# Differential attention scores as three fp32r passes instead of fp32 matmuls

## The reference

```
s = jnp.einsum('bqhcd,bkhcd->bhcqk', qblk, kk, preferred_element_type=jnp.float32) * scale
p = jax.nn.softmax(s, axis=-1)
a = p[:, :, 0] - lam_full * p[:, :, 1]
return jnp.einsum('bhqk,bkhe->bqhe', a.astype(v.dtype), v)
```

## Time and profile before

| | |
|---|---|
| median of three runs | 3787.01 us |
| the profiled execution | 3786.81 us |
| its span | 3785.0 us |
| TensorE matmuls busy | 3628.1 us, 96% |
| VectorE busy | 1748.2 us, 46% |
| ScalarE busy | 1507.0 us, 40% |
| GpSimd busy | 1277.0 us, 34% |
| first score block of the first paired layer | starts at 1882.92 us |
| first score block of the second paired layer | starts at 2849.29 us |

### The profile page before, as it was taken

One profiled execution on the slowest core, in us unless ns is written; L12 is line 12 of the kernel. 1 busy time (PEld: TensorE's weight loads), 2 busy tenths in 40 slices (PEclk: granted clock), 3 DMA queues, 4 the chain that ended last, 5 costly groups with the idle time before them and its releaser, 6 DMA issues.

```text
span 3785.0 us, 53305 instructions
## 1 busy us (share of the span) xinstructions
PE 3628.1 (96%) x19978; PEld 2921.6 (77%) x19978; DVE 1748.2 (46%) x2548; ACT 1507.0 (40%) x2525; POOL 1277.0 (34%) x540
## 2 busy tenths in 40 slices
PE   7999999999988889999999999899989999999998
PEld 5875788888866767888777778688867777877886
DVE  4766643333356655443555552511156555252114
ACT  4343432222355654332555552422235555333222
POOL 2530333222331112444423334344433333434443
PEclk9999999999999999999999999999999999999999
DMA  5358211111210001322211122222222122222222
GB/s 205 117 218 303 80 67 61 62 66 61 78 56 23 23 23 67 106 94 96 99 62 67 63 72 95 73 101 98 96 78 73 68 68 68 87 86 85 98 95 89
DMA packets 84708, 333.82 MB, mean 88 GB/s; under 512 B 9520, under 2 KB 9648, under 8 KB 78000
## 3 DMA queue, kind: packets, MB, share of 16 engines
q1 hardware_dynamic: 83808, 329.22, 24.9%
q10 hardware_dynamic: 720, 2.10, 0.2%
HBM read 329.18 MB, written 2.10 MB: 88 GB/s over the span
## 4 chain that ended last, share of the span: by engine, by line
PE 78%; issue 11%; DVE 6%; POOL 3%; ACT 2%; POOLq 0%; DVEq 0%; ACTq 0%
PE pB L276 16%; PE pB L277 16%; PE pB L278 16%; PE pB L2327 13%; POOL w_lo L2892 3%; PE pO L276 1%; PE pO L278 1%; PE pO L277 1%; PE pT L278 1%; PE pT L277 1%; PE pT L276 1%; PE pT L2385 1%; DVE arena L903 1%; DVE small L1975 1%; PE pO L2412 1%
## 5 line engine op out<-in xcount | busy, mean ns | idle before, releaser
L2892 POOL TENSOR_TENSOR w_lo<-w_raw,w_hi 128x1024 fp32r<-128x1024 f32 x520 | 1260.7, 2426 | 2356.7 <-ACT w_hi L322 2356.3
L276 PE MATMUL pB<-h_hi,w_hi 128*128 128x512 f32 x2084 | 822.7, 395 | 43.0 <-DVE h_lo L2820 15.3
L277 PE MATMUL pB<-h_lo,w_hi 128*128 128x512 f32 x2084 | 817.2, 392 | 0.0
L278 PE MATMUL pB<-h_hi,w_lo 128*128 128x512 f32 x2084 | 816.2, 392 | 0.0
L322 ACT ACTIVATE w_hi<-w_raw 128x1024 fp32r<-128x1024 f32 x520 | 547.8, 1054 | 479.9 <-PE pB L278 315.0
L276 PEld LDWEIGHTS pB<-h_hi,w_hi 128*128 128x128 f32 x2084 | 395.2, 190 | 137.0 <-issue 39.1
L278 PEld LDWEIGHTS pB<-h_hi,w_lo 128*128 128x128 f32 x2084 | 395.1, 190 | 83.5
L277 PEld LDWEIGHTS pB<-h_lo,w_hi 128*128 128x128 f32 x2084 | 395.4, 190 | 79.9 <-issue 0.7
L276 PE MATMUL pB<-b_hi,w_hi 128*128 128x512 f32 (+1 forms) x1088 | 403.3, 371 | 6.4 <-POOL w_lo L2892 6.4
L277 PE MATMUL pB<-b_lo,w_hi 128*128 128x512 f32 (+1 forms) x1088 | 398.3, 366 | 0.0
L278 PE MATMUL pB<-b_hi,w_lo 128*128 128x512 f32 (+1 forms) x1088 | 397.9, 366 | 0.0
(11 more groups left out here) (546 smaller groups left out, 5223.7 us busy)
## 6 DMA issues: line engine op xcount, KB each, us to landing
w_raw<-stream SPq DMA_DIRECT2D x520, 512.0 KB, 3.2
under<-ada SPq DMA_DIRECT2D x42, 1024.0 KB, 4.8
arena<-ada SPq DMA_DIRECT2D x6, 1024.0 KB, 17.6
x<-xT SPq DMA_DIRECT2D x1, 2048.0 KB, 8.5
out<-x SPq DMA_DIRECT2D x8, 256.0 KB, 2.1
xc<-cT SPq DMA_DIRECT2D x1, 1024.0 KB, 26.5
arena<-bmask ACTq DMA_DIRECT2D x1, 1024.0 KB, 4.8
arena<-brope ACTq DMA_DIRECT2D x2, 256.0 KB, 5.1
```

Source lines behind the costliest of these rows:

```text
L276: pe.matmul(dst, lh, rh, start=(begin and k == 0), stop=False)
L277: pe.matmul(dst, lh, rl, start=False, stop=False)
L278: last = pe.matmul(dst, ll, rh, start=False, stop=(end and k == len(pairs) - 1))
L2892: pool.tensor_tensor(w_lo[:, s, :], w_raw[:, s, :], w_hi[:, s, :].bitcast(F32), ALU.subtract).then_inc(lo_ready, 1)
```

## The change

- **Scores.** For a differential turn `pe_scores` makes, for both 64-row halves, three fp32r passes instead of one fp32 matmul: high q x high k, remainder q x high k, high q x remainder k. In block 0 it waits for `score_hi` before the first pass and for `score_lo` before the second and once more before the third, so that the key's remainder is needed last.
- **High parts.** `act_score_high`, a ScalarE copy that rounds 512 columns to fp32r. For queries it stands at the head of `act_chunk` of the key chunk, ahead of the swap (`split_behind`). For keys it stands behind chunk 1 (turn 0) or behind `act_turned` of block 3 of the turn before (turns 2, 4, 6), and waits for the rotation.
- **Remainders.** `dve_score_low`, a VectorE subtraction with both inputs in SBUF, in place over `qr` and `kr`. For queries it stands at the head of `dve_rope` of the key chunk, ahead of the rotation; for keys at its end.
- `score_parts` is a view of the arena with fp32r type; no memory is added. There are 16 of each new ScalarE and VectorE operation (2 layers, 4 turns, q and k). No DMA changes.

```diff
--- before.py
+++ after.py
@@ -164,6 +164,8 @@
         with nc.sbuf_tensor("arena", [P, ARENA], F32) as arena:
             pass
         with nc.sbuf_tensor("mla_under", [P, 5376], F32), nc.sbuf_tensor("mla_q", [P, 4, T], F32R) as mla_q, nc.sbuf_tensor("mla_k", [P, 4, TC], F32R) as mla_k:
+            pass
+        with nc.sbuf_tensor("score_under", [P, 3072], F32), nc.sbuf_tensor("score_parts", [P, 12, T], F32R) as score_parts:
             pass
         xh_hi, xh_lo = sb("xh_hi", [P, KD * C], F32R), sb("xh_lo", [P, KD * C], F32R)
         xb_hi, xb_lo = sb("xb_hi", [P, KD * C], F32R), sb("xb_lo", [P, KD * C], F32R)
@@ -2270,6 +2272,27 @@
         V_NO = [sum(kind(c)[0] == "v" for c in range(k)) for k in range(PAIR_CHUNKS)]
         N_ROPES, N_VS = 32, 16
+        def splits(k):
+            return k < PAIR_CHUNKS and kind(k)[0] != "v" and kind(k)[1] == 0 and diff(TURN_OF[k])
+        SPLIT_NO = [sum(splits(c) for c in range(k)) for k in range(PAIR_CHUNKS)]
+        N_SPLITS = sum(splits(k) for k in range(PAIR_CHUNKS))
+        def score_halves(u):
+            at = 1 if diff(u) else 2
+            return [(score_parts[:, w * 6 + at, :], score_parts[:, w * 6 + u % 2 * 3, :]) for w in range(2)]
+        def split_behind(k):
+            return [j for j in range(max(k - 2, 0), k) if splits(j) and TURN_OF[j] == TURN_OF[k]
+                    and not split_alone(j) and next(c for c in range(j + 1, PAIR_CHUNKS) if kind(c)[0] != "v") == k]
+        def split_alone(k):
+            return diff(TURN_OF[k]) and kind(k)[0] == "k"
         def turn_start(u):
             at = turn_chunks(u)[0] + turn_chunks(u)[1] if u < TURNS else PAIR_CHUNKS + EARLY - 1
@@ -2312,6 +2335,7 @@
         pair_s, pair_m, pair_e, pair_c, pair_t = sem("pair_s"), sem("pair_m"), sem("pair_e"), sem("pair_c"), sem("pair_t")
         pair_ca, pair_cd, pair_v, pair_o = sem("pair_ca"), sem("pair_cd"), sem("pair_v"), sem("pair_o")
+        score_hi, score_lo = sem("score_hi"), sem("score_lo")
         swapped, rope_step, vfm_ready, gates_ready = sem("swapped"), sem("rope_step"), sem("vfm_ready"), sem("gates_ready")
@@ -2347,14 +2371,22 @@
             first, cnt = turn_chunks(u)
             if t == 0:
                 pe.wait_ge(rope_done, l * N_ROPES + ROPE_NO[first + 2 * cnt // 3 - 1] + 1)
+                parts_ready = l * N_SPLITS + sum(splits(k) for k in range(first + cnt))
+                if diff(u):
+                    pe.wait_ge(score_hi, parts_ready)
             if n and diff((n - 1) // TB % TURNS):
                 pe.wait_ge(pair_e, n)
             elif n:
                 pe.wait_ge(pair_m, n)
             q, k = qr[par], kr[par]
+            (qh, ql), (kh, kl) = score_halves(u)
+            passes = ((qh, kh, True, False), (ql, kh, False, False), (qh, kl, False, True))
             if diff(u):
-                for c in range(2):
-                    last = pe.matmul(pS[:, each(c)], q[halves(c), 0, t * P:(t + 1) * P], k[halves(c), 0, :], start=True, stop=True)
+                for i, (q_, k_, begin, end) in enumerate(passes):
+                    if t == 0 and i:
+                        pe.wait_ge(score_lo, parts_ready - 2 + i)
+                    for c in range(2):
+                        last = pe.matmul(pS[:, each(c)], q_[halves(c), t * P:(t + 1) * P], k_[halves(c), :], start=begin, stop=end)
             else:
                 near = ((0, t * P, (t + 2) * P),) if t + 1 < TB else ((0, t * P, T), (P, 0, P))
                 for o, a, b in near:
@@ -2462,6 +2494,8 @@
             if k >= PAIR_CHUNKS:
                 act.activation(sg[k - PAIR_CHUNKS], bank[s][:, :], ACT.Copy).then_inc(evac[s], 1)
             elif kind(k)[0] != "v":
+                for j in split_behind(k):
+                    act_score_high(act, l, j)
                 r = l * N_ROPES + ROPE_NO[k]
                 if r >= 2:
                     act.wait_ge(rope_done, r - 1)
@@ -2482,6 +2516,13 @@
                 act.activation(win[:, 0, 0], by_half[:, 1, TB - 1], ACT.Copy).then_inc(vfm_ready, 1)
             act_hi_part(act, g + SLOTS)
+        def act_score_high(act, l, k):
+            u = TURN_OF[k]
+            w = "qk".index(kind(k)[0])
+            act.wait_ge(rope_done, l * N_ROPES + ROPE_NO[k] + 1)
+            act.activation(score_halves(u)[w][0], (qr, kr)[w][u % 2][:, 0, :], ACT.Copy).then_inc(score_hi, 1)
         def act_values(act, l, k):
             s = (G_DIFF[l] + k) % SLOTS
             act.wait_ge(v_turned, l * N_VS + V_NO[k] + 1)
@@ -2534,6 +2575,8 @@
         def act_pairs(act, l):
             for k in range(FIRST):
                 act_chunk(act, l, k)
+                if splits(k) and split_alone(k):
+                    act_score_high(act, l, k)
             act_exps(act, l, 0, 0)
             for u in range(TURNS):
                 for t in range(TB):
@@ -2552,6 +2595,9 @@
                     if u and t == finish_at(u - 1):
                         act_finish(act, l, u - 1)
                     act_turned(act, l, u, t)
+                    if t + 1 == TB and put_off(u):
+                        for k in ropes_in(in_part(u, t - 1, 1)):
+                            act_score_high(act, l, k)
                     if t + 1 < TB:
                         act_exps(act, l, u, t + 1)
                     elif u + 1 < TURNS and not late(u + 1):
@@ -2575,6 +2621,8 @@
             dst = (qr if what == "q" else kr)[u % 2][:, gi, :]
             windowed = what == "k" and gi == 0 and not diff(u)
             to = knat if windowed else dst
+            for j in split_behind(k):
+                dve_score_low(dve, l, j)
             dve.wait_ge(swapped, r + 1)
             dve.tensor_tensor(to, bank[s][:, :], cos2, ALU.mult).then_inc(evac[s], 1)
             dve.tensor_tensor(qsw[r % 2], qsw[r % 2], sin2, ALU.mult).then_inc(rope_step, 1)
@@ -2588,6 +2636,16 @@
                 dve.tensor_tensor(win[:, 0, 0], a[:, 1, TB - 1], b[:, 1, TB - 1], ALU.add).then_inc(rope_done, 1)
             else:
                 dve.tensor_tensor(dst, dst, qsw[r % 2], ALU.add).then_inc(rope_done, 1)
+            if splits(k) and split_alone(k):
+                dve_score_low(dve, l, k)
+        def dve_score_low(dve, l, k):
+            u = TURN_OF[k]
+            w = "qk".index(kind(k)[0])
+            high, low = score_halves(u)[w]
+            dve.wait_ge(score_hi, l * N_SPLITS + SPLIT_NO[k] + 1)
+            dve.tensor_tensor(low, (qr, kr)[w][u % 2][:, 0, :], high.bitcast(F32), ALU.subtract).then_inc(score_lo, 1)
         def dve_maxima(dve, link, l, u, t):
             n = (l * TURNS + u) * TB + t
```

## The result

The changed kernel takes 3810.43 us, the median of six runs (3807.65 to 3813.71), against 3786.33 for the kernel before (six runs). The ratio is 1.0066, 95% interval 1.0053 to 1.0079: slower by about 24 us. The forecast was 3803, slower by 16, with a range up to 3820. The profiled execution took 3808.37 us.

The account below looks back on a forecast made before the run. It took TensorE, busy 96% of the span, as the bound, except in turn 0, whose end waits for VectorE. Late blocks 11.6 + turn 0 7.7 - blocks 3.2 = +16.1 us on 3786.8 gave 3803, range 3792 to 3820.

Parts of the forecast that it names:

- Block by itself: One score block without waits: 0.88 us instead of 1.06, halves side by side; 18 blocks save 3.2 us.
- The rival of halves in series: Score blocks: the two 64-row halves run one after the other, 0.51 us more a block, time 3819; chance 0.10.
- The estimate from the four-tile ratio: Score blocks: each pass stretched by a third of 0.23 us, saving used up, sum about 3 us higher.
- Late blocks: First score block of turns 2, 4 and 6: operands late, +1.93 us a turn, 11.6 us for six.
- GpSimd is out of the way: Late turns and turn 0: GpSimd's subtraction holds no VectorE operation; +1.2 us, time 3788; chance 0.15, its half included.
- Turn 0: Start of each layer: first block +2.9, second waits 1.1 more for exponentials; +3.9 us, 7.7 for two layers.
- the later blocks of turn 0: Six later score blocks of turn 0: no saving counted, since that turn's end waits for VectorE.
- The clock: Behind the new idle times: falls to 1.2 GHz, about 1.8 us each; in all eight places 3817, chance 0.10.
- a variant in turn 0 alone: Clock falls behind turn 0's new idle times only: time 3807; counted within the forecast's chance of 0.62.
- the first rival: Same as "GpSimd is out of the way": no VectorE operation held, time 3788; chance 0.15.
- its half, 3797: Late turns free of GpSimd but turn 0 held: 5.9 + 7.7 - 3.2, time 3797; within the chance of 0.15.
- all hidden: All differential score blocks: no operand is late, 32 x -0.18 = -5.8 us, time 3781; chance 0.03.

Follow-up runs that it names:

- Experiment 4: Changed kernel, but in turns 2, 4 and 6 the query's remainder subtraction reads its first operand from PSUM instead of SBUF: 3802.00 us, ratio 1.0035 to the kernel before.
- experiment 5: Changed kernel, but for turns 2, 4 and 6 the query's copy and subtraction moved ahead into blocks 2 and 3 of the turn before: 3798.15 us, ratio 1.0027.
- Experiment 6: Changed kernel, but in turn 0 the high-part copies stand behind the key's swap and the remainders behind both rotations: 3799.38 us, ratio 1.0030.
- Experiment 3: Changed kernel with six full-size filler matmuls in TensorE's idle time ahead of the first score block of turns 2, 4 and 6: 3806.35 us, ratio 1.0052.
- experiment 2: Changed kernel with the new copies and subtractions kept, but scores as the old fp32 matmuls waiting for the rotation only: 3802.26 us, ratio 1.0039.
- 7: Changed kernel with both moves: query operations of turns 2, 4 and 6 moved ahead, and turn 0's copies and remainders reordered: 3786.04 us, ratio 0.9998.
- 9: Changed kernel, nothing moved on ScalarE or VectorE, with nine products ahead of the first score block of turns 2, 4 and 6: 3803.55 us, ratio 1.0044.

## Why the prediction was right

- *Block by itself*: 0.88 forecast, 0.90 measured; halves side by side, third pass 0.23 behind the second. 18 blocks gave about 3.1 us (3.2 forecast). The rival of halves in series is out. The estimate from the four-tile ratio of the Trainium skill ("TensorE: Matmul & The Clock Gate", "Measured speedup vs the span model") does not hold for two halves here: no pass is stretched.
- *Late blocks*: +1.93 forecast. A turn in which the clock stayed up is +1.80 up to the late block's start and 0.05 more inside it, 1.85; six are 11.1 (11.6 forecast). The parts fit as well: the subtraction takes 1.47 (1.58 forecast; GpSimd starts 0.52 later than before and not 0.63), the third pass is 0.1 late (0.15). Experiment 4 shows that GpSimd holds the subtraction, experiment 5 that the two query operations make 1.4 of the 1.8 us. The rival "GpSimd is out of the way" is out.
- *Turn 0*: +3.9 forecast. The first block is 2.86 late (2.9 forecast). In the one layer with this turn 0 where the clock stayed up (experiment 5) the second block waits 1.0 for exponentials (1.1 forecast) and turn 1 starts 3.8 later than before; two are 7.6 (7.7 forecast). In the changed kernel the clock fell in both layers, TensorE came 0.5 us after the exponentials, and turn 1 starts 4.2 later. So the slow clock mostly took the time of a wait that would have stood there, and added 0.4 a layer. Experiment 6 takes all of it back, and 0.35 a layer more: the later blocks of turn 0, counted at nothing, do gain a little.
- *Sum without the clock*: 11.1 + 7.6 - 3.1 = 15.6, forecast 16.1. Experiment 3, which keeps the clock up outside turn 0, has +16.5 with the 0.9 of turn 0 in it.
- *The clock* is the term that was mis-sized. It stood among the rivals, at 0.10 for all eight places (+14) and as a variant in turn 0 alone (+3.6), and at nothing in the sum. It fell at four of the six late blocks, at one of the two old waits, where the forecast had no place for it, and twice in turn 0. Outside turn 0 a fall cost 1.5 to 1.6 us (1.8 forecast), 7.6 together, and in turn 0 it cost 0.9 for both: 8.5 in all. It should have been in the sum at about half its full price: a stall of 1.8 us in this stream costs about 2.9 on average.
- 15.6 + 8.5 = 24.1, as in the traces (+24.1) and between the medians (+24.1).
- *Slips in the working*: 2.9 + 1.1 - 0.18 is 3.8 and not 3.9 (the sum used 7.7 for two, which is right). The chances call all of the first rival "same", but its half, 3797, lies 10 us up and would be slower; and "all hidden", 5.8 us down, lies within the 7.6 us and would be the same, not faster.

Not settled: what decides whether the clock falls behind a given idle time (below).

## What to carry to other kernels

When an operand is split so that TensorE has less to do, count what the split puts in front of the first use, on the engines' queues and in order; here 0.17 us a block was won and 1.8 us a turn lost. A VectorE operation with both inputs in SBUF is not a 0.7 us operation when it is issued while GpSimd subtracts: put it where GpSimd is idle, or have the operation in that slot read PSUM. And do not price a wait of TensorE at its length alone: here 1.8 us cost 2.9 on average, because the clock fell behind two waits of three. Fill it with products that are due anyway, after a look at who waits for what those products delay.

## What the runs showed of the hardware

- How often the granted clock fell to half behind an idle time of TensorE, over all traces (idle as the records give it). Late blocks: 1.7 us, eight of twelve (changed kernel and experiment 6); 1.0, none of six (experiment 2); 0.9, one of six (experiment 4); 0.3, none of twelve (experiments 5 and 7). The old wait of 1.6 us: eight of 22, none of them in the kernel before. Turn 0: 2.8 us, nine of ten (changed kernel, experiments 3, 4, 5 and 9); 2.0, one of two (experiment 2). In the kernel before the clock stayed up behind 2.21 us. So the length of the gap alone doesn't decide.
- VectorE's subtraction of one PSUM and one SBUF operand, issued while GpSimd subtracts, takes 0.68 us; with two SBUF operands 1.47 at the same place, and it ends 0.55 us behind GpSimd's. The rotation's addition in turn 0, issued 0.2 us into GpSimd's subtraction, takes 2.73 to 2.76 and ends as far behind.
- fp32r matmuls of 64 rows by 512 columns run in pairs on the two row halves: six in 0.90 us with the changes of shape, where four fp32 records took 1.06.
